# Chunk inverse of an RWKV-7 layer: one product group for eight heads instead of two for four

## What is computed

```python
def step(S, inp):
    r_t, w_t, k_t, v_t, kk_t, a_t = inp
    sa = jnp.einsum('bhvk,bhk->bhv', S, -kk_t)
    S = (S * w_t[:, :, None, :] + sa[..., None] * (kk_t * a_t)[:, :, None, :]
         + v_t[..., None] * k_t[:, :, None, :])
    return S, jnp.einsum('bhvk,bhk->bhv', S, r_t)
```

## Time and profile before

| what | value |
|---|---|
| median of 3 runs | 2711.51 us (2709.19 to 2714.97) |
| profiled execution, its own time | 2712.11 us |
| its span in the profile | 2710.3 us |
| busy PE / PEld / DVE / ACT / POOL | 94% / 90% / 39% / 18% / 40% |
| recurrence stage | about 1097 to 1344 us |
| one chunk of that stage, in the steady middle | 28.16 us |

### The profile page before, as it was taken

How to read it: one execution, slowest core, us unless ns; L and a number is a source line. 1 busy time by engine, 2 the same in 40 slices (tenths; PEclk the granted TensorE clock), 3 DMA queues, 4 the chain that set the end, 5 groups by cost and what they waited for, 6 DMA issues and landing times.

```text
span 2710.3 us, 49309 instructions
## 1 busy us (share of the span) xinstructions
PE 2545.1 (94%) x19899; PEld 2441.1 (90%) x19899; DVE 1068.1 (39%) x1905; ACT 492.6 (18%) x1006; POOL 1090.4 (40%) x864
## 2 busy tenths in 40 slices
PE   5999999999999999788868899889999999999997
PEld 4999999999999998688727899758999999999997
DVE  6332133213362574577474511623533213321323
ACT  4110011001130213333323320222211001100102
POOL 3444444444454443222144373004444444444442
PEclk8999999999999999799968999989999999999999
DMA  3111111111132111000112151323111111111111
GB/s 113 47 46 47 47 46 46 47 47 46 37 118 64 44 28 58 2 3 3 46 63 101 42 160 54 113 76 98 44 47 46 47 47 46 46 47 47 46 39 74
DMA packets 220700, 150.42 MB, mean 55 GB/s; under 512 B 10831, under 2 KB 211113, under 8 KB 219946
## 3 DMA queue, kind: packets, MB, share of 16 engines
q1 hardware_dynamic: 217546, 132.67, 16.3%
q10 hardware_dynamic: 2560, 16.09, 1.6%
q0 software_dynamic: 480, 0.05, 0.0%
HBM read 134.73 MB, written 14.04 MB: 55 GB/s over the span
## 4 chain that ended last, share of the span: by engine, by line
PE 89%; DVE 6%; ACT 2%; issue 2%; DMA 1%; SPq 0%; POOL 0%; DVEq 0%; ACTq 0%; POOLq 0%
PE bank L385 26%; PE bank L387 26%; PE bank L386 26%; PE bank L1787 1%; PE bank L1278 1%; PE bank L1756 1%; PE bank L1287 1%; PE bank L1820 1%; PE bank L1254 1%; DVE TT L1191 0%; DVE y_nat L1979 0%; DVE Ti L1177 0%; ACT prob L1843 0%; PE bank L1351 0%; DVE PM L1161 0%
## 5 line engine op out<-in xcount | busy, mean ns | idle before, releaser
L358 POOL TENSOR_TENSOR w_hi<-raw,cst 128x512 fp32r<-128x512 f32 x366 | 465.3, 1271 | 1227.1 <-PE bank L387 1050.1
L385 PE MATMUL bank<-h_hi,w_lo 128*128 128x344 f32 x2856 | 918.8, 322 | 8.9 <-issue 7.5
L387 PE MATMUL bank<-h_hi,w_hi 128*128 128x344 f32 x2856 | 913.1, 320 | 0.0
L386 PE MATMUL bank<-h_lo,w_hi 128*128 128x344 f32 x2856 | 912.5, 320 | 0.0
L363 POOL TENSOR_TENSOR w_lo<-raw,w_hi 128x512 fp32r<-128x512 f32 (+1 forms) x398 | 526.1, 1322 | 64.9 <-ACT w_hi L355 35.2
L385 PEld LDWEIGHTS bank<-h_hi,w_lo 128*128 128x128 f32 x2856 | 536.1, 188 | 17.2 <-issue 14.4
L386 PEld LDWEIGHTS bank<-h_lo,w_hi 128*128 128x128 f32 x2856 | 535.1, 187 | 2.7 <-issue 0.5
L387 PEld LDWEIGHTS bank<-h_hi,w_hi 128*128 128x128 f32 x2856 | 536.1, 188 | 1.2
L387 PE MATMUL bank<-hid_hi,w_hi 128*128 128x344 f32 x1056 | 337.3, 319 | 0.0
L385 PE MATMUL bank<-hid_hi,w_lo 128*128 128x344 f32 x1056 | 337.2, 319 | 0.0
L386 PE MATMUL bank<-hid_lo,w_hi 128*128 128x344 f32 x1056 | 337.1, 319 | 0.0
(11 more groups left out here) (312 smaller groups left out, 2830.4 us busy)
## 6 DMA issues: line engine op xcount, KB each, us to landing
raw<-in_ffn_gate SPq DMA_DIRECT2D x88, 256.0 KB, 2.8
raw<-in_ffn_up SPq DMA_DIRECT2D x88, 256.0 KB, 2.9
raw<-in_ffn_down SPq DMA_DIRECT2D x80, 256.0 KB, 2.7
raw<-in_w_in SPq DMA_DIRECT2D x44, 256.0 KB, 2.8
cache<-in_cache_mem_k SPq DMA_DIRECT2D x8, 1024.0 KB, 4.9
cache<-in_cache_mem_v SPq DMA_DIRECT2D x8, 1024.0 KB, 4.9
x_save<-x ACTq DMA_DIRECT2D x1, 4128.0 KB, 12.5
x<-x_save ACTq DMA_DIRECT2D x8, 516.0 KB, 6.5
```

What stands on the lines that cost most here:

```text
L358: nc.gpsimd.tensor_tensor(w_hi[part], raw[part], cst[:, C_ONE:C_ONE + 1, 0:ph["width"]].to_broadcast([P, nk, ph["width"]]), ALU.mult)\
L385: nc.tensor.matmul(out, b, hi, start=first, stop=False)
L386: nc.tensor.matmul(out, a, lo, start=False, stop=False)
L387: m = nc.tensor.matmul(out, a, hi, start=False, stop=last)
```

## The change

At every level the two halves are taken together. `y_tensor` and `d_tensor` lose their argument `hp`: one group of 16 products (32 instructions in the trace) into one bank. `flip_vector`, `y_vector` and `d_vector` become one instruction each on twice the width. Every wait is for both halves, and every step raises its semaphore by two, so all other counts stay as they are. The first flip moves behind the second half's `level0_vector`. The number of products, their operands and the amount of data are the same.

```diff
-        def y_bank(m, lv, hp):
-            return turn(m, 8 + 4 * (lv - 1) + hp)
+        def y_bank(m, lv):
+            return turn(m, 8 + 4 * (lv - 1))
...
-        def y_vector(dve, m, lv, hp):
-            k = 10 * m + 2 * (lv - 1) + hp
-            dve.wait_ge(S("Y_t"), k + 1)
-            dve.wait_ge(S("D_t"), max(k - 1, 0))
-            nc.vector.tensor_tensor(Ym[:, hp], y_bank(m, lv, hp)[:, 0:256].rearrange(
-                "p (h t) -> p h t", h=4), low_mask(lv), ALU.mult).then_inc(S("Y_ev"), 1)
+        def flip_vector(dve, m, lv):
+            dve.wait_ge(S("T_made"), 12 * m + 2 * lv)
+            dve.wait_ge(S("Y_t"), 10 * m + 2 * (lv - 1))
+            nc.vector.transpose(Ti[:, :].rearrange("p a h t -> p (a h t)"),
+                                TT[m % 2][:, :].rearrange("p a h t -> p (a h t)")).then_inc(S("T_flip"), 2)
+
+        def y_vector(dve, m, lv):
+            k = 10 * m + 2 * (lv - 1)
+            dve.wait_ge(S("Y_t"), k + 2)
+            dve.wait_ge(S("D_t"), k)
+            nc.vector.tensor_tensor(heads(Ym), y_bank(m, lv)[:, :].rearrange("p (h t) -> p h t", h=8),
+                                    low_mask(lv), ALU.mult).then_inc(S("Y_ev"), 2)
+
+        def d_vector(dve, m, lv):
+            dve.wait_ge(S("D_t"), 10 * m + 2 * lv)
+            t = second(heads(TT[m % 2]), lv)
+            nc.vector.tensor_tensor(t, t, d_bank(m, lv)[:, 0:256].rearrange(
+                "p (h j b) -> p h j b", h=8, b=1 << lv), ALU.add).then_inc(S("T_made"), 2)
...
                 level0_vector(dve, m, 0)
-                flip_vector(dve, m, 1, 0)
                 pair_vector(dve, m, 0, 1)
                 level0_vector(dve, m, 1)
-                flip_vector(dve, m, 1, 1)
+                flip_vector(dve, m, 1)
...
-                for hp in (0, 1):
-                    y_vector(dve, m, lv, hp)
+                y_vector(dve, m, lv)
                 if lv == 2 and n >= 0:
                     state_vector(dve, n, 1)
-                for hp in (0, 1):
-                    d_vector(dve, m, lv, hp)
-                    if lv < NLV:
-                        flip_vector(dve, m, lv + 1, hp)
+                d_vector(dve, m, lv)
+                if lv < NLV:
+                    flip_vector(dve, m, lv + 1)
...
-        def y_tensor(pe, m, lv, hp):
-            pe.wait_ge(S("T_flip"), 10 * m + 2 * (lv - 1) + hp + 1)
-            for ht in range(4):
-                for ck in (0, 1):
...
+        def y_tensor(pe, m, lv):
+            pe.wait_ge(S("T_flip"), 10 * m + 2 * lv)
+            for hp in (0, 1):
+                for ht in range(4):
+                    for ck in (0, 1):
...
-                y_tensor(pe, m, 1, 0)
-                pe.wait_ge(S("tok_ev"), 3 * m + 2)
-                y_tensor(pe, m, 1, 1)
+                y_tensor(pe, m, 1)
```

More of the change, by code:

```diff
@@ L961, in mask, with low_mask, heads, d_bank @@
             return cst[:, table:table + 1, CH * part:CH * part + CH].to_broadcast([P, n, CH])
-        def low_mask(lv):
-            return mask(C_LVL + (lv - 1) // 2, (lv - 1) % 2, 4)
+        def low_mask(lv, n=8):
+            return mask(C_LVL + (lv - 1) // 2, (lv - 1) % 2, n)
         def second(a, lv):
             return a.rearrange("p h (j u b) -> p h j u b", u=2, b=1 << lv)[:, :, :, 1, :]
+        def heads(a):
+            return a.rearrange("p a h t -> p (a h) t")
         def turn(m, k):
             return bank[LB[(28 * m + k) % 3]]
-        def y_bank(m, lv, hp):
-            return turn(m, 8 + 4 * (lv - 1) + hp)
-        def d_bank(m, lv, hp):
-            return turn(m, 10 + 4 * (lv - 1) + hp)
+        def y_bank(m, lv):
+            return turn(m, 8 + 4 * (lv - 1))
+        def d_bank(m, lv):
+            return turn(m, 10 + 4 * (lv - 1))
         def ends(a, n):
@@ L1272, in token_tensor, with d_tensor @@
             i.then_inc(S("tok"), 1)
-        def y_tensor(pe, m, lv, hp):
-            pe.wait_ge(S("T_flip"), 10 * m + 2 * (lv - 1) + hp + 1)
-            for ht in range(4):
-                for ck in (0, 1):
[L1278 to L1291, removed]
+        def y_tensor(pe, m, lv):
[3 more added lines that the diff above has]
+                    for ck in (0, 1):
+                        i = mmul(y_bank(m, lv)[half(ck), (4 * hp + ht) * CH:(4 * hp + ht + 1) * CH],
+                                 PM[m % 2][half(ck), 0, hp, 0, ht, :], Ti[half(ck), hp, ht, :],
+                                 start=True, stop=True)
+            i.then_inc(S("Y_t"), 2)
+        def d_tensor(pe, m, lv):
+            pe.wait_ge(S("Y_ev"), 10 * m + 2 * lv)
+            for hp in (0, 1):
+                for ht in range(4):
+                    for ck in (0, 1):
+                        i = mmul(d_bank(m, lv)[half(ck), (4 * hp + ht) * 32:(4 * hp + ht + 1) * 32].rearrange(
+                                     "p (j b) -> p j b", b=1 << lv),
+                                 Ym[half(ck), hp, ht, :], second(TT[m % 2][half(ck), hp], lv)[:, ht],
+                                 start=True, stop=True)
+            i.then_inc(S("D_t"), 2)
         def mv_tensor(pe, m):
@@ L1404, in chunk_tensor @@
                 pe.wait_ge(S("tok_ev"), 3 * m + 3)
-                d_tensor(pe, m, 1, 0)
-                d_tensor(pe, m, 1, 1)
-                y_tensor(pe, m, 2, 0)
-                y_tensor(pe, m, 2, 1)
+                d_tensor(pe, m, 1)
+                y_tensor(pe, m, 2)
             if n >= 0:
@@ L1412, in chunk_tensor @@
             if m < 8:
-                d_tensor(pe, m, 2, 0)
-                d_tensor(pe, m, 2, 1)
-                y_tensor(pe, m, 3, 0)
-                y_tensor(pe, m, 3, 1)
+                d_tensor(pe, m, 2)
+                y_tensor(pe, m, 3)
                 mv_tensor(pe, m)
-                d_tensor(pe, m, 3, 0)
-                d_tensor(pe, m, 3, 1)
-                y_tensor(pe, m, 4, 0)
-                y_tensor(pe, m, 4, 1)
+                d_tensor(pe, m, 3)
+                y_tensor(pe, m, 4)
                 out_v_tensor(pe, m)
-                d_tensor(pe, m, 4, 0)
-                d_tensor(pe, m, 4, 1)
-                y_tensor(pe, m, 5, 0)
-                y_tensor(pe, m, 5, 1)
-                d_tensor(pe, m, 5, 0)
-                d_tensor(pe, m, 5, 1)
+                d_tensor(pe, m, 4)
+                y_tensor(pe, m, 5)
+                d_tensor(pe, m, 5)
         SMP = [lambda ht: smp_w[:, ht, :], lambda ht: nkk[:, ht, SEQ:T], lambda ht: smp_b[:, ht, :],
```

## The result

The change makes the kernel slower: 2843.8 us median (2823.1 to 2856.4) against 2711.3 (2709.2 to 2715.0) measured beside it, a ratio of 1.048 with a 95% interval of 1.041 to 1.055. The sign was forecast; the size was not. 132.5 us were added, where 28 were expected and 46 was the end of the range. The four executions after differ by 33 us, with mean granted clocks from 0.934 (the shortest) to 0.913 (the longest).

What follows compares the result with a forecast made beforehand. The ring of waits between PE and DVE was taken to bound the kernel. Profiled 2712.1 + 19.5 for serial levels + 8.4 for clock falls = 2740.0, median 0.6 below: 2739 us; range 2725 to 2757.

Steps and rivals of the forecast that it cites:

- The ring between PE and DVE: Recurrence stage: neither engine is full in a 28.16 us chunk; the length of their mutual waits sets the time.
- The serial levels: Recurrence levels: add, flip, Y, copy, D run one after another, 4.24 us a level; +2.44 us per chunk, +19.5 in all.
- level 1: First level, Y start to next Y start: 3.38 us becomes 4.24, +0.86; u products on PE stay hidden.
- level 4: Fourth level, Y start to next Y start: 3.68 us becomes 4.24, +0.56.
- set-up: Chunk start: moving the first flip lets half 1's copy to `PM` start earlier, -0.37 us; the flip itself hides.
- The hand-overs: Gaps between engine steps in a level: flip to Y 0.05, copy to D 0.05, PE to DVE 0.02, add to flip 0.03.
- The clock: PE's clock falls in about half of the chunks, 4 x 2.1 = 8.4 us; the two earlier falls cost 1.14 and 3.07.
- No further falls: Rival: the clock falls no more often than before, only the 19.5 us are added; 2731 us, chance 0.23.
- A fall in every chunk: Rival: every chunk loses 3.07 us to the clock; 2756 us, chance 0.18 shared with high Vector prices.
- Flat Vector prices: Rival: merged DVE instructions cost what a half costs (copy 0.42, flip 0.45, add 0.29); 2710 us, chance 0.06.
- the other bound of the unknown prices: DVE flips 0.90, adds 0.57, copies 0.84: +2.0 us per chunk, 2747 without falls; with some falls, within a shared 0.18.
- Vector as the bound: Rival: only DVE's occupied time counts, so fewer instructions save about 13 us; 2698 us, chance 0.05.

Runs made afterwards that it cites:

- the coupling alone: Kernel before, instructions left at half width, but every wait is for both halves, adds ahead of flips, first flip moved as in the change; 2852.1 us, 1.052.
- the run with the small fill: Changed kernel plus useless 64-column matmuls on PE: four behind D of levels 1 to 4, two behind Y of level 5, some in first chunk; 2751.3 us, 1.015.
- useless multiply: Kernel before, halves uncoupled, plus one useless 128x256 multiply on DVE behind the flips of each level; 2740.8 us, 1.012.

## Why the prediction was right, and where it was wrong

**The bound and the mechanism: right.** The ring between PE and DVE set the time, the halves did hide each other, and the coupling alone costs what the whole change costs. The wide instructions cost what was estimated (0.711, 0.692, 0.421 for 0.71, 0.67, 0.42), the flip's by scaling from the copy.

**The serial levels: right in kind, 1.85 us per chunk short.** At the full clock, in the run with the small fill:

| term | forecast | measured |
|---|---|---|
| level 1 | +0.86 | 4.59 - 3.38 = +1.21 |
| level 2 | +0.63 | 4.95 - 4.15 = +0.80 |
| level 3 | +0.43 | 4.63 - 3.81 = +0.82 |
| level 4 | +0.56 | 4.52 - 3.68 = +0.84 |
| level 5 | +0.33 | 1.99 - 1.56 = +0.43 |
| set-up (first pair products to first Y) | -0.37 | (1215.82 - 1207.14) - (1204.14 - 1195.65) = +0.19 |
| chunk | +2.44 | 32.45 - 28.16 = +4.29 |

The hand-overs carry about half of it: I took the length of a group as the time to its end (1.15, 1.12, with 0.02 behind), where the consumer started 1.25 and 1.24 after the group's start, and 0.03 between add and flip, which measured 0.09 (0.51 - 0.42); 0.24 of the 0.28 by which level 4 is longer than the forecast 4.24. Before, these gaps were read where the other half's work covered them. In level 1 the u products, which I held to be hidden, end last. The set-up is the largest single term, 0.56 of the 1.85: the second pair products did come earlier (by 0.45, 3.44 against 3.89 behind the first), but from them to Y it is 0.64 longer. I priced the move by one wait and didn't follow the two behind it, GpSimd's product and the copies that PE's token products wait for (0.43). Over 8 chunks: 34 us instead of 19.5.

**The clock: the step that failed.** "I expect such falls in about half of the chunks, at the mean of the two prices" gave 8.4 us. With 34 of the 132 us for the ring, some 98 were the clock's. Both factors were wrong, and the second more: every chunk was hit, and the low clock was not an interlude of 1.1 to 3.1 us but 44.4 us of 47.8, at 15.35 per chunk. The first chunk had no fall at all: its clock was low from the start and did not come back. The two falls before each ended within a chunk; I carried this price over to a ring that was to be looser. I read the stretch from 1124, too, as Y and D groups, where it holds one D group. The text named this outcome ("one that stays at 0.50 through whole chunks, then above the range") but gave it no case, no price and no chance. The rows had a price for it: the pair products of the last chunk took 1.69 instead of 1.10; PE's 24.67 us of a chunk stretched in that ratio are 37.9, 13.2 more, and 8 x (13.2 + 2.44) = 125 us, close to the 132 measured. That it is so close is in part luck: at 0.50 from end to end the same group takes 1.98, and the ring's 2.44 was too small. Without this case the range ended at 46.

Against how much longer a chunk is at the full clock, what the clock then adds (the last two columns are estimates, with the steady chunk's price for all eight):

| kernel | full-clock chunk | over 28.16 | time over before | 8 chunks of it | the rest, the clock |
|---|---|---|---|---|---|
| useless multiply | 29.25 | +1.09 | +29.3 | 8.7 | 20.6 |
| copy merged | 29.65 | +1.49 | +45.8 | 11.9 | 33.9 |
| all merged | 32.45 (with fill) | +4.29 | +132.5 | 34.3 | 98.2 |

In these three, the whole loss is 3.4 to 3.9 times what the looser chunk costs by itself. What in PE's activity decides is not settled by these runs; that the products are the same and only their spacing differs is shown by the coupled and the delayed kernel.

**The rivals.** No further falls: refuted, and its 19.5 us were too few. A fall in every chunk: right in its count, by far too cheap. Flat Vector prices: refuted by 0.711, 0.692 and 0.421, and the other bound of the unknown prices by the same three. Vector as the bound: refuted; in the 32.45 us of the filled chunk DVE is busy for 19.84 and idles 1.29 ahead of an add. The rule of the Trainium skill behind that rival (VectorE: DVE Perf Modes, section Rules for kernel authors) is not borne out here: 15 instructions fewer per chunk, and the same 47.8 us as with all of them, because what the wide instructions save on DVE (0.18 in level 3) they give back by starting later.

## What to carry to other kernels

Two halves that alternate between two engines hide more than their instructions' lengths say: price a merge by the measured start of the consumer behind the whole group, not by the group's length. Where TensorE waits in a ring with another engine, give the clock a case of its own, in which the whole stage runs at 1.2 GHz, priced from groups seen at that level; a ring that got looser by 1.09 us per chunk of 28.16 already lost 29 us, where the delay itself was 9. If such a stage can't be made tighter, a few useless matmuls in PE's idle time show what the clock costs, and here gave back 93 of 132 us, which still leaves the kernel slower than before; work that is already there, moved into those gaps, might do it at no cost, which was not tried.

## What the runs showed of the hardware

- The granted clock can be low nearly throughout a stage in which no idle time of PE is long: in the middle chunk of after the longest wait of PE is 1.40 us, and PE is busy for 40.83 of 47.80 us. PE's busy share does not warn of it (24.67 of 28.16 before, at 1.00), since slow products are busy, too. The Trainium skill (TensorE: Matmul & The Clock Gate, section A second HAM failure mode: psum-queue depth-cycling) tells of a kernel in which frequent short idle times between groups of matmuls let the clock swing. The trace agrees as far as the clock rises and falls once per chunk, for 3.40 us; that the short idle times are the cause is not shown, since the chunk before has them as well (0.39 to 0.40 ahead of Y, 1.29 in the set-up) and keeps 1.00.
- The clock came back within one chunk under fill products (47.78, 37.99, 32.46 us), and was lost within one without them (36.45, 39.21, 45.46), though there the filled chunks had already lost it for a time.
- A 128x256 DVE product of two SBUF operands took 1.15 us with GpSimd's 1.27 us product beside it for 0.86, 0.68 with 0.40 beside it, and 0.43 with nothing; the pair copy beside it, with one operand from PSUM, kept its length (0.65 at 1198.84, within GpSimd's 1198.66 to 1199.92). The Trainium skill (GPSIMD Engine Reference, section 1. Specifications) says that GpSimd shares its SBUF interfaces with the Vector engine's instructions that have two inputs there; the trace agrees.
- Two neighbouring half-width copies occupy DVE for 0.75 us, one merged copy for 0.69: merging saves 0.06 on DVE and delays the first half's result by 0.27 (0.69 against 0.42).
